# First layer of a two-block transformer kernel on one core: gate projection, compressed softmax and output weights moved in the order of four engines

## The reference, cut

```python
q, kc, vc, ks, vs, kw, vw, gate, z = jnp.split(u @ w_in, points, axis=-1)
gate = jax.nn.sigmoid(gate).reshape(b, s, G, J, 3)
k_cmp, v_cmp = compress(kc, pe_k, w1_k, w2_k), compress(vc, pe_v, w1_v, w2_v)
...
p_c = jax.nn.softmax(jnp.where(m_c, s_c, NEG), axis=-1) * jnp.any(m_c, axis=-1)[:, None]
...
o = gate[..., 0:1] * o_c + gate[..., 1:2] * o_s + gate[..., 2:3] * o_w
o = o.reshape(b, s, NSA_WIDTH) * jax.nn.silu(z)
return o @ w_out
```

## Time and profile before

| what | value |
|---|---|
| median of three executions | 1403.68 us |
| profiled execution, its own time | 1405.38 us |
| its span | 1403.6 us |
| mean granted TensorE clock | 0.987 |
| busy: TensorE, ScalarE, GpSimd, VectorE | 1346.3, 747.4, 764.0, 658.6 us |

### The profile page before, as it was taken

One profiled execution on the slowest core, in us unless ns is written; L12 is line 12 of the kernel. 1 busy time (PEld: TensorE's weight loads), 2 busy tenths in 40 slices (PEclk: granted clock), 3 DMA queues, 4 the chain that ended last, 5 costly groups with the idle time before them and its releaser, 6 DMA issues.

```text
span 1403.6 us, 20936 instructions
## 1 busy us (share of the span) xinstructions
PE 1346.3 (96%) x7738; PEld 1101.8 (79%) x7738; DVE 658.6 (47%) x1609; ACT 747.4 (53%) x1572; POOL 764.0 (54%) x786
## 2 busy tenths in 40 slices
PE   6999999998999999999999999999999999999997
PEld 5878778886888787878788888778889887778885
DVE  4352566766251444554330011881463347887135
ACT  4252388888343465665442333892534355887252
POOL 4452257665753555665553525687546534586652
PEclk9999999999899999999999999999999999999999
DMA  6242011111424322221343232424226322002322
GB/s 245 94 151 91 15 32 61 40 37 61 165 80 133 133 75 77 89 79 58 150 180 120 92 110 98 144 98 167 104 73 222 113 88 64 1 16 101 140 91 60
DMA packets 28901, 138.66 MB, mean 99 GB/s; under 512 B 3584, under 2 KB 4096, under 8 KB 18048
## 3 DMA queue, kind: packets, MB, share of 16 engines
q1 hardware_dynamic: 15200, 98.05, 19.9%
q10 hardware_dynamic: 13600, 39.27, 8.1%
HBM read 127.86 MB, written 8.39 MB: 97 GB/s over the span
## 4 chain that ended last, share of the span: by engine, by line
PE 79%; DVE 7%; ACT 6%; POOL 4%; issue 2%; DMA 2%; SPq 0%; POOLq 0%; ACTq 0%; DVEq 0%
PE psum L523 47%; PE psum L557 10%; PE psum L1459 4%; PE psum L1487 3%; PE psum L1416 3%; PE psum L1507 2%; DVE w_free L1568 2%; PE psum L1070 2%; POOL w_lo L478 2%; PE psum L1044 2%; PE psum L766 1%; PE psum L1472 1%; POOL w_free L1699 1%; ACT w_free L956 1%; ACT x_r L1628 1%
## 5 line engine op out<-in xcount | busy, mean ns | idle before, releaser
L478 POOL TENSOR_TENSOR w_lo<-w_raw,w_hi 128x512 fp32r<-128x512 f32 (+3 forms) x153 | 392.4, 2580 | 277.5 <-ACT w_hi L467 268.2
L467 ACT ACTIVATE w_hi<-w_raw 128x2048 fp32r<-128x2048 f32 (+1 forms) x89 | 158.5, 1781 | 91.2 <-DMA w_raw<-in_weights 77.2
L523 PE MATMUL psum<-w_hi,split 128*128 128x512 f32 x608 | 197.7, 399 | 4.0 <-POOL w_lo L478 4.0
L523 PE MATMUL psum<-u_lo,w_hi 128*128 128x512 f32 (+1 forms) x428 | 169.9, 397 | 2.1 <-POOL w_lo L478 2.1
L523 PE MATMUL psum<-u_hi,w_hi 128*128 128x512 f32 (+1 forms) x428 | 167.8, 392 | 0.0
L523 PE MATMUL psum<-u_hi,w_lo 128*128 128x512 f32 (+1 forms) x428 | 167.7, 392 | 0.0
L956 ACT ACTIVATE w_free<-w_free,neg_max 128x512 f32<-128x512 f32 (+3 forms) x256 | 148.3, 584 | 11.4 <-DVE neg_max L1568 10.3
L523 PEld LDWEIGHTS psum<-w_hi,split 128*128 128x128 f32 x608 | 116.0, 191 | 29.0 <-POOL w_lo L478 5.0
L523 PE MATMUL psum<-w_hi,u_lo 128*128 128x512 f32 (+2 forms) x352 | 134.4, 382 | 2.1 <-DVE u_lo L916 1.8
L523 PE MATMUL psum<-w_lo,u_hi 128*128 128x512 f32 (+2 forms) x352 | 132.6, 377 | 0.0
L523 PE MATMUL psum<-w_hi,u_hi 128*128 128x512 f32 (+2 forms) x352 | 132.6, 377 | 0.0
(11 more groups left out here) (237 smaller groups left out, 2787.4 us busy)
## 6 DMA issues: line engine op xcount, KB each, us to landing
w_raw<-in_weights SPq DMA_DIRECT2D x83, 1024.0 KB, 4.8
x<-x_scratch ACTq DMA_DIRECT2D x12, 512.0 KB, 4.9
w_raw<-in_weights SPq DMA_DIRECT2D x10, 512.0 KB, 4.0
gain<-in_gains ACTq DMA_DIRECT2D x9, 512.0 KB, 5.0
gain<-in_strips ACTq DMA_DIRECT2D x16, 256.0 KB, 2.8
spare<-in_strips ACTq DMA_DIRECT2D x16, 256.0 KB, 2.9
x_scratch<-x ACTq DMA_DIRECT2D x8, 512.0 KB, 4.0
gain<-in_near ACTq DMA_DIRECT2D x8, 512.0 KB, 4.3
```

The source lines that it names most:

```text
L467: high = nc.scalar.activation(w_hi[b][:, c], w_raw[b][:, c], ACT.Copy)
L478: low = nc.gpsimd.tensor_tensor(w_lo[b][:, c], w_raw[b][:, c], w_hi[b][:, c].bitcast(F32), ALU.subtract)
L523: mm = nc.tensor.matmul(dst, lhs, rhs, start=(a == 0 and k == 0 and (wl, ul) == (0, 1)), stop=(a + 1 == u and k + 1 == nk and (wl, ul) == ...
```

## The change

It has five parts.

1. The gates' unit and products go between cmp0 and cmp1. The low part of cmp1's weights is made by VectorE (`compress_weights_low`) in place of GpSimd, with a semaphore of its own; GpSimd's next split counts for both.
2. The compressed scores of the last two groups go between the products of k's first unit, and the softmax runs in two halves of 128x1024, each with its own Exp.
3. The z chunks: 12 ahead of step 0 (8 before the turns of the compressed probabilities, 4 after), 4 in each of rounds 0 and 2, then 2 per round, until step 46. They stand between the values and the second turn of a round. The first tile is taken before the attention begins, the others at ScalarE's steps 3, 9, 17, 25, 33, 41 and 49 (before: 3, 11, 19, ... 59), and a fourth place holds z tiles (gain[1], whose load moves behind the attention).
4. ScalarE splits both first units of nsa_out in quarters at steps 51 to 58; GpSimd subtracts them in eighths at steps 53 to 68.
5. ScalarE's z_high_part and GpSimd's z_low_part follow the new steps.

```diff
+_run("nsa_gate", 1, (8,), GATES, "features")
 _run("nsa_cmp1", 1, (16,), 128, "compress")
-_run("nsa_gate", 1, (8,), GATES, "features")
...
+        def compress_weights_low(dve):
+            n = RUNS["nsa_cmp1"]["unit"]
+            b = SLOT[n]
+            dve.wait_ge(w_high, n + 1)
+            nc.vector.tensor_tensor(w_lo[b][:], w_raw[b][:], w_hi[b][:].bitcast(F32), ALU.subtract).then_inc(cmp1_low, 1)
...
-        Z_FIRST = 6
+        Z_FIRST, Z_EARLY = KC + KC // 2, KC // 2
         def z_step(t):
-            return max(0, KC * (t + 1) - Z_FIRST - 1) // 2 * 2 + 1
+            return 1 if t == 1 else KC * t - 9
+        def z_round(d):
+            return (Z_FIRST + Z_EARLY * d, Z_EARLY) if d < 2 else (Z_FIRST + 2 * Z_EARLY + 2 * (d - 2), 2)
...
             if f is nsa_flow:
-                z_fill(pe, 0, Z_FIRST)
+                z_fill(pe, 0, KC)
                 for g in range(3):
                     compress_turn_tensor(pe, g)
+                z_fill(pe, KC, Z_FIRST - KC)
...
                 if d >= 0:
                     values(d, 0)
                     values(d, 1)
+                if f is nsa_flow:
+                    z_fill(pe, *z_round(i // 2))
...
                 if 0 <= i + 1 - LAG < f.steps:
                     turn(i + 1 - LAG)
                 if f is nsa_flow:
-                    z_fill(pe, Z_FIRST + i, 2)
...
-                    if f.steps - 4 <= i < f.steps:
-                        split_high(act, NSA_OUT, i - f.steps + 4, 4)
+                    if 51 <= i < 59:
+                        split_high(act, NSA_OUT + (i - 51) // 4, (i - 51) % 4, 4)
...
-                    if f.steps - 3 <= i <= f.steps:
-                        split_low(pool, NSA_OUT, i - f.steps + 3)
-                    if i == f.steps + LAG + 2:
-                        split_low(pool, NSA_OUT + 1)
+                    if 53 <= i < 69:
+                        split_low(pool, NSA_OUT + (i - 53) // 8, (i - 53) % 8, 8)
...
-            for j in range(NT):
-                compress_scores_tensor(pe, 1, j)
-            project_tensor(pe, "nsa_k")
+            project_tensor(pe, "nsa_k", between={(0, 0, j): beside_first_k(pe, j) for j in range(NT)})
...
-            compress_softmax_scalar(act)
+            compress_softmax_scalar(act, 0)
             z_high_part(act, 0)
             z_high_part(act, 1)
+            compress_softmax_scalar(act, 1)
...
+            z_take(act, 0)
```

More of the change, by code:

```diff
@@ L469, in split_high, with split_low @@
                 high.then_inc(w_high, 1)
-        def split_low(pool, n, part=None, parts=4):
+        def split_low(pool, n, part=None, parts=4, count=1):
             b = SLOT[n]
@@ L479, in split_low @@
             if part in (None, parts - 1):
-                low.then_inc(w_ready, 1)
+                low.then_inc(w_ready, count)
         def next_unit(run, i, a):
@@ L1645, in pair_scalar @@
                         compress_turned_high(act, 3)
-                    for t in range(KC):
+                    for t in range(1, KC):
                         if i == z_step(t) + 2:
                             z_take(act, t)
-                        if t >= 2 and i == z_step(t - 2) + 3:
+                    for t in range(2, KC):
+                        if i == (z_step(t - 2) + 3 if t > 2 else 1):
                             z_high_part(act, t)
-                    if f.steps - 4 <= i < f.steps:
-                        split_high(act, NSA_OUT, i - f.steps + 4, 4)
+                    if 51 <= i < 59:
+                        split_high(act, NSA_OUT + (i - 51) // 4, (i - 51) % 4, 4)
                 if 0 <= i - 1 < f.steps:
@@ L1668, in pair_scalar @@
                     high(i - LAG)
-                if i == (f.steps if f is na_flow else f.steps + LAG - 1):
+                if i == (f.steps if f is na_flow else f.steps + LAG - 1) and f is not nsa_flow:
                     split_high(act, RUNS[f.name + "_out"]["unit"] + 1)
@@ L1723, in pair_pool @@
             for i in range(2, f.steps + LAG + 5):
+                if f is nsa_flow and i == 2:
+                    z_low_part(pool, 2, 0)
+                    z_low_part(pool, 2, 1)
                 if i - 2 < f.steps - (1 if f is na_flow else 0):
@@ L1919, in compress_hidden_tensor @@
             b = SLOT[run["unit"]]
-            pe.wait_ge(w_ready, run["unit"] + 1)
+            pe.wait_ge(*((cmp1_low, 1) if a else (w_ready, run["unit"] + 1)))
             for o in range(16):
@@ L2044, in beside_last_q, with beside_first_k, compress_softmax_vector @@
             return lambda: compress_scores_tensor(pe, 0, j)
-        def compress_softmax_vector(dve):
+        def beside_first_k(pe, j):
+            return lambda: compress_scores_tensor(pe, 1, j)
+        def compress_softmax_vector(dve, gp):
             def spread(off):
-                return at(off, 64).unsqueeze(2).to_broadcast([P, 64, 32])
-            pc = at(N_PC, HEADS * NT * 32).rearrange("p (h c) -> p h c", c=32)
-            for g in range(4):
+                return at(off, 32).unsqueeze(2).to_broadcast([P, 32, 32])
+            pc = at(N_PC + gp * 2 * T, 2 * T).rearrange("p (h c) -> p h c", c=32)
+            largest, r = N_MX + 32 * gp, N_MX + 64 + 32 * gp
+            for g in (2 * gp, 2 * gp + 1):
                 dve.wait_ge(cmp_s, g + 1)
@@ L2057, in compress_softmax_vector @@
             settle("dve", dve)
-            done("dve", nc.vector.tensor_reduce(at(N_MX, 64), pc, AX, ALU.max))
+            done("dve", nc.vector.tensor_reduce(at(largest, 32), pc, AX, ALU.max))
             settle("dve", dve)
-            nc.vector.tensor_tensor(pc, pc, spread(N_MX), ALU.subtract).then_inc(cmp_shifted, 1)
-            dve.wait_ge(cmp_exp, 1)
-            r = at(N_MX + 64, 64)
-            done("dve", nc.vector.tensor_reduce(r, pc, AX, ALU.add))
+            nc.vector.tensor_tensor(pc, pc, spread(largest), ALU.subtract).then_inc(cmp_shifted, 1)
+            dve.wait_ge(cmp_exp, gp + 1)
+            done("dve", nc.vector.tensor_reduce(at(r, 32), pc, AX, ALU.add))
             settle("dve", dve)
-            done("dve", nc.vector.reciprocal(r, r))
+            done("dve", nc.vector.reciprocal(at(r, 32), at(r, 32)))
             settle("dve", dve)
-            g0 = gate[:].rearrange("p (t g j b) -> p g t j b", t=NT, g=4, j=4)[:, :, :, :, 0]
-            by_tile = r.rearrange("p (g t j) -> p g t j", g=4, t=NT)
-            dve.wait_ge(bank_free["act"], 4 + RUNS["nsa_gate"]["taken"] + 4)
+            g0 = gate[:].rearrange("p (t g j b) -> p g t j b", t=NT, g=4, j=4)[:, 2 * gp:2 * gp + 2, :, :, 0]
+            by_tile = at(r, 32).rearrange("p (g t j) -> p g t j", g=2, t=NT)
+            dve.wait_ge(bank_free["act"], 4 + RUNS["nsa_cmp1"]["taken"] + 4)
             done("dve", nc.vector.tensor_tensor(by_tile, by_tile, g0, ALU.mult))
@@ L2515, in _ @@
             first_scalar(act)
-            load_gain(act, 1)
             load_compress(act)
@@ L2546, in _ @@
             act.wait_ge(nsa_flow.gated, 2 * KC)
+            load_gain(act, 1)
             chain_scalar(act, diff_chain, "nsa_out", A["x"])
@@ L2615, in _ @@
             first_pool(pool)
-            for name in ("nsa_v", "nsa_kc", "nsa_q0", "nsa_cmp0", "nsa_cmp1", "nsa_gate", "nsa_q1"):
+            for name in ("nsa_v", "nsa_kc", "nsa_q0"):
+                project_pool(pool, name)
+            split_low(pool, RUNS["nsa_q1"]["unit"], count=2)
+            for name in ("nsa_cmp1", "nsa_q1"):
                 project_pool(pool, name)
```

38 lines of the change are left out of this document (21 added, 17 removed).

## The result

The changed kernel takes 1410.45 us (median of 5 runs, 1408.99 to 1413.97) against 1403.68 (1401.01 to 1405.08): ratio 1.0061, 95% interval 1.0048 to 1.0074. It is 6.8 us slower; +4.7, which is 1408.4, was forecast. The profiled execution took 1410.45 us with a span of 1408.6, mean granted clock 0.992.

The account below looks back on a forecast made before the run. TensorE was taken to bound the first layer's attention. The terms -3.7 + 6.9 + 10 + 3.3 - 11.8 gave +4.7, so 1403.7 became 1408.4 us; range 1395 to 1416, the forecast's own 1403 to 1413.

Parts of the forecast that it names:

- Front: Gates, cmp1 and q1: the wait for w_lo before q1 is only split, 0 us; bounds -1.8 and +2.3.
- Scores: Last two groups' scores spread into k's first unit run at full clock; z starts near 159.4, gain 3.7 us.
- Start: Start of the attention: ten more z chunks add 6.8 us, waits and slow clock nearly unchanged; net +6.9 us.
- Steps 8 to 47: Attention rounds: five z takes each cost TensorE 2.0 us net, +10, and three clock falls add 3.3 us.
- Steps 48 to the end: Attention's end to first output product: earlier nsa_out split and departed z chunks gain 11.8 us; bounds 5 and 15.
- The rest: After the first output product: 0 us; the moved load_gain(1) lands 5 us later, well before y is normed.
- (a): Rival on steps 8 to 47: the take is hidden anyway, their wait and clock terms vanish; 1395.1 us, chance 0.20.
- (b): Rival on steps 8 to 47: the waits come but the clock holds; 1405.1 us, chance 0.22.
- (c): Rival on the attention's end: it stays long without z, half of the 11.8 is kept; 1414.3 us, chance 0.20.
- (d): Rival on the z takes: every table load drains as well, each wait 1.4 us longer; 1415.3 us, chance 0.02.

Follow-up runs that it names:

- experiment 3: The kernel before with only the last two groups' scores between k's first-unit products and the softmax in halves; 1399.77 us, ratio 0.9981.
- experiment 7: The changed kernel with nsa_out's first units split at the old, later steps (60 to 64, 66 and 69); 1417.06 us, ratio 1.0093 to the kernel before.
- Experiment 1: The changed kernel with the z chunks put back behind the second turn of a round, pace and takes kept; 1406.90 us, ratio 1.0030 to the kernel before.
- experiments 4: The changed kernel with z tiles 2 to 7 taken one ScalarE step earlier; 1416.82 us, ratio 1.0098 to the kernel before.
- experiment 5: The changed kernel with Copy in place of Silu in the z take, so without its table loads; 1395.51 us, ratio 0.9946 to the kernel before.
- experiment 2: The changed kernel with 14 z chunks ahead and two per round: 1397.74 us with chunks between values and second turn, 1394.89 with chunks at the round's end.
- first kernel of experiment 2: The changed kernel with 14 z chunks ahead and two per round, chunks still between values and second turn; 1397.74 us, ratio 0.9962 to the kernel before.
- experiment 6: The faster kernel with 14 chunks ahead and chunks at the round's end, changed to 12 ahead, two per round; 1417.05 us, ratio 1.0098 to the kernel before.

## Why the prediction was right, point by point

- **Front, 0.** Measured +0.3. VectorE's subtract ran from 93.35 for 2.29 us (forecast 93.2, 2.29), and ended before GpSimd's began at 96.20. The wait ahead of q1 was split, but the other way round: 0.81 at cmp1 (forecast 1.1) and 1.12 at q1 (forecast 0.7).
- **Scores, -3.7.** Measured -3.8, the z product at 159.60 (forecast 159.4); alone (experiment 3) -3.8 in the stretch itself and -3.4 between the medians.
- **Start, +6.9.** Measured +5.1. The wait at the first z product of round 2 is 2.78 (forecast 2.85). The step that was too large is the "1.6 for a slow stretch" behind it: the clock stayed at 1.00.
- **Steps 8 to 47, "+10, and 3.3 for the clock".** Measured +13.9. Five waits of 2.11 (forecast 2.25), 2.15 per period where the clock held (forecast 2.0), three falls of the five (forecast three), 3.1 for them together. That there were three was a guess from 1.50, 1.41 and 1.82, and that it came true was luck: in experiment 7 the same five waits were followed by two. What was wrong is the reason that I gave for the place of the chunks. I had counted the second turn behind the chunks as work that would have covered the wait. Experiment 1 shows that at this pace it wouldn't have: with the turn ahead of the chunks the period stays within 0.1 us, and the waits stand elsewhere. The mechanism of the take, with ScalarE's table load ahead of the Silu, is shown by experiments 4 and 5, and that the pace puts it into the wrong round by experiment 2.
- **Steps 48 to the end, -11.8.** Measured -8.1; I had 45.6 us for the stretch and it took 49.2. The waits themselves were nearly right: 2.83 in round 50 (2.85), 1.27 behind GpSimd (1.8), 7.9 in all with the small ones (7.3; the waits that the prediction lists add up to 7.6, so its own gain should have read 11.5). The terms that were off are the clock, which I took as full and which lost 1.5 behind the 2.83 (0.97 over 49.2 us), and the 38.3 of work, which is 39.8. Restarts behind the waits that remain may be the reason for that last 1.5; no run shows it. GpSimd's eighths took 0.73, not 0.65.
- **The rest, 0.** -2.4 in the profiled execution, from three places in later layers (1.2 between 667 and 722 us, 0.6 between 1068 and 1178, 0.5 between 1194 and 1307). The change touches nothing there, and the medians are 6.8 apart where the two profiled executions are 5.1 apart. The largest of the three holds a fall of the clock: in the kernel before a wait of 2.47 at 682.39 is followed by four us at 0.57, and the changed kernel has full clock there. The same stretch took between 1030.6 and 1034.3 us over all the profiled kernels up to the last product. I take it as scatter.

Of the rivals, (a), the take hidden anyway, is out with five waits of 2.11. (b), the clock holds, was right for two waits of five and for the one at the start, and what decides between them is open. (c), the end stays long, was right in part: of the 11.8 there were 8.1. (d) is out: the Silu starts 1.30 behind the start of its load (193.06 and 194.36), and in experiment 5, without loads, the wait fell by 1.42, about one load. The Trainium skill (ScalarE: Activation LUTs, "What ACT_TABLE_LOAD costs") has a DRAIN of 1380 ns beside the 1283 of the load for every switch. By that rule a switch is 2.66 us, and taking it away would have taken away the whole 2.11; the trace agrees with the 1283 alone.

The sum came out nearer than its terms, and that is luck: 1.8 too much was charged at the start, 3.7 too little at the end, and the later layers gave 2.4 back in the profiled execution. The term that carries the forecast, the five waits with their falls, is the one that came as laid out.

## What to carry to other kernels

When a step that reloads tables is tied to the end of a tile, the pace at which tiles are filled decides which round it falls into. Look at what stands behind it on its own engine in each round, not only for where the waiting engine has other work to put first. Three paces were tried here, and only the one of the kernel before let the step pass nearly free. Going back to it, with 14 chunks ahead and two per round in place of 12 and four in each of the first two rounds, kept the earlier split (worth 6 us) and took 13 us off the changed kernel, and putting the chunks back at the round's end another 3. And when long covered work leaves a stretch, as the z products left the end, count what it covered: of 6.8 us moved, only 2 were gained there.

## What the runs showed of the hardware

The granted clock does not follow from a wait's length alone. The five waits of 2.11 or 2.12 us at the same place, before the same work, were followed by half clock in three cases in one kernel and in two in another (experiment 7), and the wait of 2.78 at the start by none in the changed kernel, by 0.68 over four us in that of experiment 7 and, as 2.79, by 0.61 in the first kernel of experiment 2. The rows of experiment 7 behind 2.78 and behind the first two of the five waits:

```profile
177.00:181.00 4.00, 3.99 (x12) 3.10 (x13) 0.00 (x0) 2.05 (x5) 0.00 (x0) 0.68 0.01 4
196.30:200.30 4.00, 3.93 (x31) 3.26 (x32) 1.44 (x3) 3.94 (x9) 0.49 (x1) 1.00 0.00 0
221.30:225.30 4.00, 3.99 (x22) 3.36 (x24) 1.04 (x2) 3.53 (x8) 2.33 (x4) 0.69 0.00 0
```

Short waits in a row are no safeguard either: those of experiment 1 (0.56, 0.65, 0.27, 0.30) were followed by no fall in five periods, those of experiment 6 (0.46, 0.73, 0.82) by one in five. Breaking the wait up was still worth 4 us over the five periods in experiment 1, in periods of nearly the same length where the clock held. What decides between the cases of equal wait stays open.
